# Up products of the last two layers 512 columns wide in pairs of PSUM banks, with fixed banks for the down products

## The chip, the cores and the metric

The kernel runs on one core of a Trainium2 chip. The metric is the device time of one execution in microseconds (us). Engines are PE (TensorE), DVE (VectorE), ACT (ScalarE), POOL (GpSimd) and SP (SyncE, which issues the DMAs).

## What is computed

256 tokens with D = 1024 go through one block with sparse attention, retention and a convolved feed-forward part, and then through a two-layer block with differential attention, a convolution, a Fourier branch and a gated feed-forward part. The change touches the feed-forward parts and the output mixing:

```python
x = x + (gate_a * y_a + gate_b * y_b) @ w_mix_out[layer]   # first block
...
x = x + merged @ w_out[l]                                   # second block, l = 0, 1
h2 = rmsnorm(x, norm2_g[l])
f_gate, f_up = jnp.split(h2 @ w_ffn_in[l], 2, axis=-1)
x = x + (jax.nn.silu(f_gate) * f_up) @ w_ffn_out[l]
```

The feed-forward width is 2816, that is 22 tiles of 128 columns for the gate and 22 for the up part. All data are float32.

## The kernel before

**Precision.** A float32 operand is split into an upper part in a shorter format (`hi`, a copy) and the rest (`lo` = value - `hi`). A product of two such operands is three products of the parts: `hi` by `hi`, `hi` by `lo`, `lo` by `hi`. Weights come from memory in chunks of 128 x 2048 (1 MB), in the order of `PLAN`. For each chunk i, SP loads `raw` (4 buffers), ACT copies it to `whi` (L913, 3 buffers), and DVE subtracts to `wlo` (L1474, 3 buffers). `splits(i + AHEAD)` with AHEAD = 2 puts that work two chunks ahead of PE in the program of ACT and DVE. The upper split of chunk i waits until PE has used chunk i - 3.

**Order.** Each engine has a program of its own (`pe_program`, `act_program`, `dve_program`, `pool_program`, `sp_program`), written in the order in which it runs. Engines wait for one another by named events that stand for values of semaphores. The program is run once in rehearsal to learn these values.

**Banks.** PSUM has eight banks of 512 float32 columns: `pb`, a ring of four that `take_bank` hands out in turn, and four (`sc`, `tp`, `ob`) for scores, transposes and values. `take_bank` makes PE wait until the earlier holder of the bank is freed (event `free`).

**Up stages.** `ffn(n, ...)` runs three times: n = 0 in the first block (`up0`, with a causal convolution), n = 1 and 2 in the second (`up1`, `up2`). Unit f of an up stage is one chunk, which holds the 128 gate columns and the 128 up columns of tile f for all 8 blocks of 128 rows. `feats` (L509 to L511) computes it on PE with the weights as stationary operand and the 256 tokens as moving operand: 8 blocks x 2 halves x 3 products of 256 columns, into one bank, gate in columns 0 to 255 and up part in 256 to 511. For n = 1 and 2, ACT then takes the SiLU of the gate half into `fs` (L1179), and DVE multiplies it by the up half into `fg` (L1880), which frees the bank. ACT makes the upper half `ghi` (L962), and DVE the lower half `glo` (L1507). `fs`, `fg` and `fu` have two buffers each.

For n = 0, ACT copies with scale and bias into `fu` (L1182), DVE does the other taps from PSUM (L1871), which frees the bank, ACT takes the SiLU (L1163), and POOL multiplies (L1389).

**Down stages.** `dn` n has 11 chunks, each of two blocks of 128 rows and all 1024 output columns. Four groups (token half tt by column half hf) accumulate over all 22 blocks, with three products of 512 columns a block each (L456 to L458 in `mul3`). Each group takes a bank of the ring at its first product, so the four groups begin with the banks of the last four up units.

**Mixing.** `yb` has four units f. DVE multiplies by the gate into `gm` (L1829), POOL adds this to `mg` (L1383), ACT makes the upper part `mh` (L962), DVE the lower part `ml` (L1507). Then `to_x` computes the product with `w_mix_out` (`mo`) from rows: PE waits for the event `mixed`, which is set once for the row blocks 0 to 3 and once for 4 to 7. In the second block DVE does that addition (L2076) itself, after the multiplication (L2071); the product there is `out0` and `out1`.

## Time and profile before

| | us |
|---|---|
| median of 3 runs (range) | 1431.55 (1429.74 to 1433.89) |
| the profiled execution's own time | 1431.48 |
| its span, first to last instruction | 1430.2 |

The page gives busy time and share of the span for each engine. The mean granted TensorE clock was 0.981 of full speed. In a timeline row the first number is the start from the beginning of the span, the second the duration, and the brackets at the end give the time in which the engine sat idle before it and what it then waited for. A row without brackets started straight after the one before it on its engine. Successive instructions of one engine overlap a little, so that a start can lie before the end of the one before.

### The profile page before, as it was taken

How to read it: one execution, taken by the hardware profiler on the slowest of the kernel's cores; microseconds unless marked ns; L12 is line 12 of the kernel's file. 1: busy time of each engine (PE TensorE's matmuls, PEld its weight loads, DVE VectorE, ACT ScalarE, POOL GpSimd, SP SyncE). 2: the span in 40 equal slices, each digit the busy share in tenths (PEclk: the TensorE clock that was granted, in tenths of full speed). 3: DMA queues.
4: the chain of work that ended last, by engine and by line, in shares of the span. 5: the costliest groups of instructions: out<-in, count | busy, mean ns of one | idle time of the engine just before them, and what ended most of it. 6: DMA issues, size and time to landing. Idle time of an engine off the chain costs nothing. (4 is left out here: it accounts for less than half of the span.)

```text
span 1430.2 us, 21050 instructions
## 1 busy us (share of the span) xinstructions
PE 1347.8 (94%) x8946; PEld 1218.7 (85%) x8946; DVE 902.4 (63%) x1173; ACT 656.4 (46%) x902; POOL 164.7 (12%) x118
## 2 busy tenths in 40 slices
PE   7999999989998898899998999999889999899999
PEld 6878889889986796678997999879667899799987
DVE  5655465568774559976576555445997657655543
ACT  5634435355553453344644444344334564444432
POOL 0100030113330005200110000000620011000000
PEclk9999999999998999999999999999999999999999
DMA  8643234444554454223344555556322334355551
GB/s 333 220 183 131 89 104 177 176 154 171 177 177 167 158 209 148 88 89 118 126 170 162 179 187 190 181 176 210 147 89 88 118 133 162 148 183 189 189 178 58
DMA packets 33503, 226.49 MB, mean 158 GB/s; under 512 B 3713, under 2 KB 4097, under 8 KB 7425
## 3 DMA queue, kind: packets, MB, share of 16 engines
q1 hardware_dynamic: 33408, 225.14, 43.9%
q8 instruction: 71, 1.16, 0.3%
q14 instruction: 24, 0.19, 0.0%
HBM read 224.08 MB, written 1.05 MB: 157 GB/s over the span
## 5 line engine op out<-in xcount | busy, mean ns | idle before, releaser
L1474 DVE TENSOR_TENSOR wlo<-raw,whi 128x2048 fp32r<-128x2048 f32 x205 | 470.9, 2300 | 305.2 <-ACT whi L913 236.8
L509 PE MATMUL ps<-hhi,whi 128*128 128x256 f32 x1696 | 490.6, 289 | 2.9 <-DVE hlo L1507 2.2
L510 PE MATMUL ps<-hlo,whi 128*128 128x256 f32 x1696 | 483.4, 285 | 0.0
L511 PE MATMUL ps<-hhi,wlo 128*128 128x256 f32 x1696 | 483.2, 285 | 0.0
L913 ACT ACTIVATE whi<-raw 128x2048 fp32r<-128x2048 f32 x205 | 388.7, 1900 | 166.2 <-PE ps L458 146.8
L509 PEld LDWEIGHTS ps<-hhi,whi 128*128 128x128 f32 x1696 | 329.0, 194 | 15.5 <-issue 13.9
L510 PEld LDWEIGHTS ps<-hlo,whi 128*128 128x128 f32 x1696 | 329.3, 194 | 0.4 <-issue 0.2
L511 PEld LDWEIGHTS ps<-hhi,wlo 128*128 128x128 f32 x1696 | 328.9, 194 | 0.0
L1353 POOL TENSOR_TENSOR st<-st,sm 128x1 f32<-128x1 f32 (+2 forms) x30 | 46.2, 1540 | 694.3 <-DVE st L1526 367.3
L456 PE MATMUL ps<-whi,hhi 128*128 128x512 f32 (+1 forms) x272 | 110.9, 408 | 8.2 <-DVE hlo L1507 6.3
L456 PE MATMUL ps<-whi,ghi 128*128 128x512 f32 x264 | 104.2, 395 | 7.1 <-DVE fu L1871 7.0
L1944 DVE SCALAR_TENSOR_TENSOR cv<-gp,sm,cv 128x256 f32<-128x256 f32 x240 | 110.4, 511 | 0.0
L457 PE MATMUL ps<-wlo,hhi 128*128 128x512 f32 (+1 forms) x272 | 107.3, 395 | 0.0
L458 PE MATMUL ps<-whi,hlo 128*128 128x512 f32 (+1 forms) x272 | 107.0, 393 | 0.0
L457 PE MATMUL ps<-wlo,ghi 128*128 128x512 f32 x264 | 103.7, 393 | 0.0
L458 PE MATMUL ps<-whi,glo 128*128 128x512 f32 x264 | 103.7, 393 | 0.0
L1179 ACT ACTIVATE fs<-ps 128x256 f32<-128x256 f32 x44 | 16.9, 383 | 145.3 <-PE ps L511 145.3
L456 PEld LDWEIGHTS ps<-whi,hhi 128*128 128x128 f32 x272 | 52.9, 194 | 21.2 <-DVE wlo L1474 4.0
L1305 ACT ACTIVATE E<-ps,st 128x256 f32<-128x256 f32 x64 | 29.7, 469 | 83.4 <-DVE st L2020 83.4
L456 PEld LDWEIGHTS ps<-whi,ghi 128*128 128x128 f32 x264 | 50.1, 190 | 18.8 <-DVE fu L1871 8.1
L458 PEld LDWEIGHTS ps<-whi,hlo 128*128 128x128 f32 x272 | 52.8, 194 | 11.0
L457 PEld LDWEIGHTS ps<-wlo,hhi 128*128 128x128 f32 x272 | 52.8, 194 | 9.6 <-issue 0.2
(267 smaller groups left out, 1784.4 us busy)
## 6 DMA issues: line engine op xcount, KB each, us to landing
raw<-in_w SPq DMA_DIRECT2D x203, 1024.0 KB, 4.8
gain<-in_rows SPq DMA_DIRECT2D x5, 512.0 KB, 3.7
raw<-in_w SPq DMA_DIRECT2D x8, 256.0 KB, 6.6
raw<-in_w SPq DMA_DIRECT2D x2, 560.0 KB, 8.0
...
```

The source lines that it names most:

```text
L456: pe.op.matmul(o, sh, mh, start=start, stop=False, skip_group_check=True)
L457: pe.op.matmul(o, sh, ml, start=False, stop=False, skip_group_check=True)
L458: signalled(pe.op.matmul(o, sl, mh, start=False, stop=stop, skip_group_check=True), names)
L509: pe.op.matmul(o, wh[:, k, c:c + 128], hi[:, k, :], start=first, stop=False, skip_group_check=True)
L510: pe.op.matmul(o, wh[:, k, c:c + 128], lo[:, k, :], start=False, stop=False, skip_group_check=True)
L511: ins = pe.op.matmul(o, wl[:, k, c:c + 128], hi[:, k, :], start=False, stop=last, skip_group_check=True)
L913: act.op.activation(t.whi[i % NHL][:, 0:n], t.raw[i % NRAW][:, 0:n], ACT.Copy).then_inc(*at("act_hi", ("hi", i)))
L1179: act.op.activation(t.fs[f % 2][:, :], ps[:, 0, :], ACT.Silu).then_inc(*at("act_out", ("fs", n, f)))
L1305: act.op.activation(t.E2[u % 2][:, c, :], t.sc[u % 2][:, c * S:c * S + S], ACT.Exp, bias=nm[:, hd, tt, c:c + 1], accum_out=lw[:, hd, tt, c ...
L1353: pool.op.tensor_tensor(o, a, small(t, "mhalf")[:, 0:a.shape[-1]], ALU.pow).then_inc(*at("pool_small", name))
L1474: dve.op.tensor_tensor(t.wlo[i % NHL][:, c], t.raw[i % NRAW][:, c], t.whi[i % NHL][:, c].bitcast(F32), ALU.subtract).then_inc(*at("dve_lo" ...
L1944: ins = dve.op.scalar_tensor_tensor(t.cv[:, f, :], t.gp[:, f, j:j + S], cw[:, f, j:j + 1], t.cv[:, f, :], ALU.mult, ALU.add)
```

## The change

- In `up1` and `up2` a unit takes a pair of banks, `b` and `b + 1`, with `b = f % 4 * 2`, so four pairs over all eight banks. `hhi` and `hlo` become the halves of one tile `hh`. For each row block and half, one product of the upper weights with both parts of the data (512 columns: columns 0 to 255 by `hhi`, 256 to 511 by `hlo`), and one of the lower weights with `hhi` (256 columns, added to columns 0 to 255).
- ACT copies the two right halves (512 columns) out into `fu`; DVE adds them to the left halves in PSUM (`summed`); ACT then takes the SiLU. The product and its two halves follow, `glo` one unit later than before.
- The four groups of every down stage have banks 4 to 7.
- The addition of `yb` moves from POOL to DVE.
- The event `mixed` is set for each pair of row blocks, for `mo`, `out0` and `out1`.

```diff
@@ -160,14 +160,31 @@
 class Banks:
 
 
+
     def __init__(self, known):
-        self.known, self.turn, self.of, self.holds = known, 0, {}, [None] * 4
+        self.known, self.ring, self.of, self.holds = known, [0, 1, 2, 3], {}, [None] * 8
 
     def take(self, name):
-        b = self.turn % 4
-        self.turn += 1
+        b = self.ring.pop(0)
+        self.ring.append(b)
+        return b, self.fix(name, b)
+
+    def fix(self, name, b):
+
         before, self.holds[b], self.of[name] = self.holds[b], name, b
-        return b, before
+        return before
+
+    def pair(self, name, b):
+
+        return self.fix(name, b + 1), self.fix(name, b)
+
...
 
     def find(self, name):
         return 0 if self.known is None else self.known[name]
@@ -265,8 +282,8 @@
     t.whi = [at(f"whi{i}", 32 + 8 * i, [128, CW], R32) for i in range(NHL)]
     t.wlo = [at(f"wlo{i}", 56 + 8 * i, [128, CW], R32) for i in range(NHL)]
     t.x = at("x", 80, [128, 2, D])
-    t.hhi = at("hhi", 88, [128, 8, S], R32)
-    t.hlo = at("hlo", 96, [128, 8, S], R32)
+    t.hh = at("hh", 88, [128, 2, 8, S], R32)
+    t.hhi, t.hlo = t.hh[:, 0, :, :], t.hh[:, 1, :, :]
     t.gain = at("gain", 104, [128, D])
     t.sm = at("sm", 108, [128, NSMALL])
     p0 = 108 + (NSMALL * 4 + 1023) // 1024
@@ -354,7 +371,8 @@
     t.mg.append(at("mg2", z + 16, [128, 8, S]))
     t.osq = at("osq", y, [128, D])
 
-    t.ps = [ctx.enter_context(nc.psum_tensor(f"ps{i}", [128, 512], F32)) for i in range(8)]
+    t.psum = ctx.enter_context(nc.psum_tensor("ps", [128, 8, 512], F32))
+    t.ps = [t.psum[:, i, :] for i in range(8)]
     t.pb, t.sc, t.tp, t.ob = t.ps[0:4], t.ps[4:6], t.ps[6], t.ps[7]
     return t
 
@@ -513,6 +531,25 @@
                 if last:
                     ins.then_inc(*at("pe_weights", ("got", u, p), *([("used", i)] if p == pairs - 1 else [])))
                 yield
+
+    def wide_feats(u, b, data):
+
+
+        i = UNITS[u][0]
+        wh, wl = weights(i, t.whi[i % NHL]), weights(i, t.wlo[i % NHL])
+        pe.wait_ge(*on("lo", i))
+        for before in pb.pair((u, 0), b):
+            if before:
+                pe.wait_ge(*on("free", before))
+        for k in range(8):
+            for w in data(k):
+                pe.wait_ge(*on(*w))
+            for f in range(2):
+                o, c = t.ps[b + f], slice(f * 128, f * 128 + 128)
+                pe.op.matmul(o[:, :], wh[:, k, c], t.hh[:, :, k, :], start=k == 0, stop=False, skip_group_check=True)
+                ins = pe.op.matmul(o[:, 0:S], wl[:, k, c], t.hhi[:, k, :], start=False, stop=k == 7,
+                                   skip_group_check=True)
+        ins.then_inc(*at("pe_weights", ("got", u, 0), ("used", i)))
 
     def norm_turned(norm, tt):
         for h in range(2):
@@ -729,7 +766,7 @@
     def to_x(u, m, norm):
 
 
-        data = lambda k, tt: ("mixed", u, k // 4)
+        data = lambda k, tt: ("mixed", u, k // 2 * 2)
         run(rows(f"{u}_0" if u != "mo" else "mo0", t.mh[m], t.ml[m], data))
         u1 = f"{u}_1" if u != "mo" else "mo1"
         run(rows(u1, t.mh[m], t.ml[m], data, held_steps(u1, 0), {13: lambda: norm_turned(norm, 0)}))
@@ -741,7 +778,10 @@
     def ffn(n, norm, after, early):
         ev.name("pe_turned", ("up starts", n, "pe"))
         for f in range(NFT):
-            run(feats(f"up{n}_{f}", *h, 8, of_norm_feats(norm)))
+            if n:
+                wide_feats(f"up{n}_{f}", f % 4 * 2, of_norm_feats(norm))
+            else:
+                run(feats(f"up{n}_{f}", *h, 8, of_norm_feats(norm)))
         banks = {}
 
         def down(i, k, kg, tt, hf, ends=()):
@@ -749,9 +789,12 @@
             pe.wait_ge(*on("g", n, kg))
             wh, wl = weights(i, t.whi[i % NHL]), weights(i, t.wlo[i % NHL])
             if kg == 0:
-                banks[tt, hf] = take_bank((f"dn{n}", tt, hf))
+                banks[tt, hf] = 4 + 2 * tt + hf
+                before = pb.fix((f"dn{n}", tt, hf), banks[tt, hf])
+                if before:
+                    pe.wait_ge(*on("free", before))
             ends = list(ends) + ([("got", f"dn{n}", tt, hf)] if kg == NFT - 1 else [])
-            mul3(t.pb[banks[tt, hf]][:, :], t.ghi[:, kg, tok(tt)], t.glo[:, kg, tok(tt)], wh[:, k, half(hf)],
+            mul3(t.ps[banks[tt, hf]][:, :], t.ghi[:, kg, tok(tt)], t.glo[:, kg, tok(tt)], wh[:, k, half(hf)],
                  wl[:, k, half(hf)], kg == 0, kg == NFT - 1, ends)
 
         chunks = UNITS[f"dn{n}"]
@@ -889,7 +932,7 @@
     st = t.st
 
     def bank(name):
-        return t.pb[pb.find(name)]
+        return t.ps[pb.find(name)]
 
     upto = [0]
 
@@ -1164,20 +1207,28 @@
                 *at("act_small", ("fs", n, f)))
 
         def out(f):
+            if n:
+                b = pb.find((f"up{n}_{f}", 0))
+                if f >= 1:
+                    g_upper(f - 1)
+                act.wait_ge(*on("got", f"up{n}_{f}", 0))
+                if f >= 2:
+                    act.wait_ge(*on("summed", n, f - 2))
+                act.op.activation(t.fu[f % 2][:, :, :], t.psum[:, b:b + 2, S:2 * S], ACT.Copy).then_inc(
+                    *at("act_out", ("low part", n, f)))
+                act.wait_ge(*on("summed", n, f))
+                if f >= 2:
+                    act.wait_ge(*on("fg", n, f - 2))
+                act.op.activation(t.fs[f % 2][:, :], t.ps[b][:, 0:S], ACT.Silu).then_inc(*at("act_out", ("fs", n, f)))
+                return
             ps = bank((f"up{n}_{f}", 0))[:, :].rearrange("p (f s) -> p f s", f=2)
-            if n == 0:
-                if f >= 2:
-                    g_upper(f - 2)
-                if f >= 1:
-                    gated(f - 1)
-            elif f >= 1:
-                g_upper(f - 1)
+            if f >= 2:
+                g_upper(f - 2)
+            if f >= 1:
+                gated(f - 1)
             act.wait_ge(*on("got", f"up{n}_{f}", 0))
             if f >= 2:
                 act.wait_ge(*on("g", n, f - 2))
-            if n:
-                act.op.activation(t.fs[f % 2][:, :], ps[:, 0, :], ACT.Silu).then_inc(*at("act_out", ("fs", n, f)))
-                return
             for v in range(2):
                 act.op.activation(t.fu[f % 2][:, v, :], ps[:, v, :], ACT.Identity, scale=fc[:, f, v, 2:3],
                                   bias=fc[:, f, v, 3:4]).then_inc(*at("act_out", *([("fu biased", f)] * v)))
@@ -1376,12 +1427,6 @@
             *at("pool_small", ("sg gained", tt)))
     for k in range(4):
         power(("ret rs", k), st[:, 200 + 2 * k:202 + 2 * k], st[:, 192 + 2 * k:194 + 2 * k], ("ret var", k))
-    for f in range(4):
-        j = 2 * f
-        pool.wait_ge(*on("free", (f"yb{f}", 0)))
-        pool.wait_ge(*on("ya gated", f))
-        pool.op.tensor_tensor(t.mg[0][:, j:j + 2, :], t.mg[0][:, j:j + 2, :], t.gm[4 + f], ALU.add).then_inc(
-            *at("pool_small", ("merged", "mo", j)))
     for tt in range(2):
         norm_power("n1", tt)
     for f in range(NFT):
@@ -1444,7 +1489,7 @@
     upto = [0]
 
     def bank(name):
-        return t.pb[pb.find(name)]
+        return t.ps[pb.find(name)]
 
     def pair(name):
         return bank(name)[:, :].rearrange("p (f s) -> p f s", f=2)
@@ -1818,7 +1863,7 @@
 
     def mixed_lower(u, j, m):
         jj = slice(j, j + 2)
-        lower([("mixed", u, j // 4)] * (j % 4 == 2), t.ml[m][:, jj, :], t.mg[m][:, jj, :], t.mh[m][:, jj, :],
+        lower([("mixed", u, j)], t.ml[m][:, jj, :], t.mg[m][:, jj, :], t.mh[m][:, jj, :],
               ("mixed hi", u, j))
 
     def yb_out(f):
@@ -1828,6 +1873,9 @@
             dve.wait_ge(*on("gm sigmoid", 2))
             dve.op.tensor_tensor(t.gm[4 + f], pair(name), t.gm[4 + f], ALU.mult).then_inc(
                 *at("dve_out", ("free", name)))
+            m = t.mg[0][:, 2 * f:2 * f + 2, :]
+            await_own("dve_out")
+            dve.op.tensor_tensor(m, m, t.gm[4 + f], ALU.add).then_inc(*at("dve_small", ("merged", "mo", 2 * f)))
             mixed_lower("mo", 2 * f, 0)
         return out
 
@@ -1872,18 +1920,35 @@
                                                 ALU.mult, ALU.add).then_inc(*at("dve_out", *ends))
                 await_own("dve_out") if j == 1 else None
 
+        def summed(f):
+
+            b = pb.find((f"up{n}_{f}", 0))
+            dve.wait_ge(*on("low part", n, f))
+            two = t.psum[:, b:b + 2, 0:S]
+            dve.op.tensor_tensor(two, two, t.fu[f % 2][:, :, :], ALU.add).then_inc(
+                *at("dve_out", ("summed", n, f)))
+
         def gated(f):
             name = (f"up{n}_{f}", 0)
-            if f:
-                g_lower(f - 1)
             dve.wait_ge(*on("fs", n, f))
-            dve.op.tensor_tensor(t.fg[f % 2][:, :], pair(name)[:, 1, :], t.fs[f % 2][:, :], ALU.mult).then_inc(
-                *at("dve_out", ("fg", n, f), ("free", name)))
+            dve.wait_ge(*on("summed", n, f))
+            if f >= 2:
+                dve.wait_ge(*on("g hi", n, f - 2))
+            dve.op.tensor_tensor(t.fg[f % 2][:, :], t.ps[pb.find(name) + 1][:, 0:S], t.fs[f % 2][:, :],
+                                 ALU.mult).then_inc(*at("dve_out", ("fg", n, f), ("free", name)))
+
+        def up_out(f):
+            if f >= 1:
+                gated(f - 1)
+            if f >= 2:
+                g_lower(f - 2)
+            summed(f)
 
         for f in range(NFT):
-            run(feats(f"up{n}_{f}", 8, lambda p: gated(f) if n else convolved(f)))
-        if n == 0:
-            g_lower(NFT - 2)
+            run(feats(f"up{n}_{f}", 8, lambda p: up_out(f) if n else convolved(f)))
+        if n:
+            gated(NFT - 1)
+        g_lower(NFT - 2)
         g_lower(NFT - 1)
         chunks = UNITS[f"dn{n}"]
         for i in chunks[:-1]:
```

How the order moves is seen best where a unit follows a unit. ACT at the start of `up1` (suffixes such as `_55` are buffers, brackets hold the semaphores that it waits for), before:

```order
L1179 ACTIVATE fs_124<-ps 128x256 [waits pe_weights]
L913 ACTIVATE whi_55<-raw_51 128x2048 [waits d_raw2]
L962 ACTIVATE ghi<-fg_126 128x256 [waits dve_out]
L1179 ACTIVATE fs_125<-ps 128x256 [waits pe_weights]
L913 ACTIVATE whi_53<-raw_52 128x2048 [waits d_raw3]
L962 ACTIVATE ghi<-fg_127 128x256 [waits dve_out]
```

and in the changed kernel:

```order
L1217 ACTIVATE fu_121<-ps 128x512 [waits pe_weights]
L1222 ACTIVATE fs_123<-ps 128x256 [waits dve_out]
L956 ACTIVATE whi_55<-raw_51 128x2048 [waits d_raw2]
L1005 ACTIVATE ghi<-fg_125 128x256 [waits dve_out]
L1217 ACTIVATE fu_122<-ps 128x512 [waits pe_weights]
L1222 ACTIVATE fs_124<-ps 128x256 [waits dve_out]
L956 ACTIVATE whi_53<-raw_52 128x2048 [waits d_raw3]
L1005 ACTIVATE ghi<-fg_126 128x256 [waits dve_out]
```

The SiLU (L1179, now L1222) waited for PE alone in the first units. It now stands behind a copy of 512 columns (L1217) and waits for DVE (`dve_out`); the upper half of `fg` (`ghi`) stands ahead of the copy.

DVE in the same place, from the first `fg` on, before:

```order
L1880 TENSOR_TENSOR fg_126<-ps,fs_124 128x256 [waits act_out]
L1474 TENSOR_TENSOR wlo_58<-raw_51,whi_55 128x2048 [waits pe_weights,act_hi,d_raw2]
L1507 TENSOR_TENSOR glo<-fg_126,ghi 128x256 [waits act_small]
L1880 TENSOR_TENSOR fg_127<-ps,fs_125 128x256 [waits act_out]
L1474 TENSOR_TENSOR wlo_56<-raw_52,whi_53 128x2048 [waits pe_weights,act_hi,d_raw3]
L1507 TENSOR_TENSOR glo<-fg_127,ghi 128x256 [waits act_small]
L1880 TENSOR_TENSOR fg_126<-ps,fs_124 128x256 [waits act_out]
```

and in the changed kernel, from the sum of unit 1 on:

```order
L1928 TENSOR_TENSOR ps<-ps,fu_122 128x2x256 [waits act_out]
L1519 TENSOR_TENSOR wlo_56<-raw_52,whi_53 128x2048 [waits pe_weights,act_hi,d_raw3]
L1937 TENSOR_TENSOR fg_126<-ps,fs_124 128x256 [waits dve_out,act_out]
L1552 TENSOR_TENSOR glo<-fg_125,ghi 128x256 [waits act_small]
L1928 TENSOR_TENSOR ps<-ps,fu_121 128x2x256 [waits act_out]
L1519 TENSOR_TENSOR wlo_57<-raw_49,whi_54 128x2048 [waits pe_weights,act_hi,d_raw0]
L1937 TENSOR_TENSOR fg_125<-ps,fs_123 128x256 [waits dve_out,act_out]
L1552 TENSOR_TENSOR glo<-fg_126,ghi 128x256 [waits act_small]
```

The sum in PSUM (L1928) is new and stands at the end of each turn, behind the lower split (L1519), `fg` (L1937) and `glo` (L1552).

PE at the first products of `dn0`, before:

```order
L456 MATMUL ps<-whi_55,ghi 128x512 [waits dve_out,dve_small,dve_lo]
L457 MATMUL ps<-wlo_58,ghi 128x512
L458 MATMUL ps<-whi_55,glo 128x512
L456 MATMUL ps<-whi_55,ghi 128x512 [waits dve_out]
L457 MATMUL ps<-wlo_58,ghi 128x512
L458 MATMUL ps<-whi_55,glo 128x512
L456 MATMUL ps<-whi_55,ghi 128x512 [waits dve_out]
L457 MATMUL ps<-wlo_58,ghi 128x512
L458 MATMUL ps<-whi_55,glo 128x512
L456 MATMUL ps<-whi_55,ghi 128x512 [waits dve_out]
```

and in the changed kernel:

```order
L474 MATMUL ps<-whi_55,ghi 128x512 [waits dve_small,dve_lo]
L475 MATMUL ps<-wlo_58,ghi 128x512
L476 MATMUL ps<-whi_55,glo 128x512
L474 MATMUL ps<-whi_55,ghi 128x512
L475 MATMUL ps<-wlo_58,ghi 128x512
L476 MATMUL ps<-whi_55,glo 128x512
L474 MATMUL ps<-whi_55,ghi 128x512
L475 MATMUL ps<-wlo_58,ghi 128x512
L476 MATMUL ps<-whi_55,glo 128x512
L474 MATMUL ps<-whi_55,ghi 128x512
```

The waits for `dve_out` ahead of the four groups, which are waits for banks, are gone; the waits for the data (`dve_small`) and the weights (`dve_lo`) stay.

## Rows read from the trace of the kernel before

**Rows 1.** Page, part 1: busy us and share of the span of each engine.

```profile
PE 1347.8 (94%) x8946; PEld 1218.7 (85%) x8946; DVE 902.4 (63%) x1173; ACT 656.4 (46%) x902; POOL 164.7 (12%) x118
```

**Rows 2.** Busy time by stage: 22 units of second up stage; engines in the page's order.

```profile
776.00:903.00 127.00, 127.00 (x1053) 126.96 (x1053) 68.59 (x65) 54.38 (x66) 0.00 (x0) 0.99 0.51 183
```

**Rows 3.** Timeline, PE, second down stage: start us, us; first and last of 24 products.

```profile
944.78 0.39 PE L456 MATMUL ps<-whi,ghi 128*128 128x512 f32 x1
...
950.00 0.39 PE L458 MATMUL ps<-whi,glo 128*128 128x512 f32 x1
```

**Rows 4.** Timeline, PE and ACT, second up stage: its first product, first SiLU.

```profile
774.52 0.55 PE L509 MATMUL ps<-hhi,whi 128*128 128x256 f32 x1 [0.84 <-DVE hlo L1507]
...
781.84 0.38 ACT L1179 ACTIVATE fs<-ps 128x256 f32<-128x256 f32 x1 [3.93 <-PE ps L511]
```

**Rows 5.** Timeline, ACT, one turn of that stage, eight units later.

```profile
827.91 0.38 ACT L1179 ACTIVATE fs<-ps 128x256 f32<-128x256 f32 x1 [3.27 <-PE ps L511]
...
828.20 1.90 ACT L913 ACTIVATE whi<-raw 128x2048 fp32r<-128x2048 f32 x1
...
830.00 0.41 ACT L962 ACTIVATE ghi<-fg 128x256 fp32r<-128x256 f32 x1
```

**Rows 6.** Timeline, DVE, the same turn.

```profile
830.19 2.29 DVE L1474 TENSOR_TENSOR wlo<-raw,whi 128x2048 fp32r<-128x2048 f32 x1 [1.43 <-ACT whi L913]
...
832.40 0.42 DVE L1507 TENSOR_TENSOR glo<-fg,ghi 128x256 fp32r<-128x256 f32 x1
...
834.09 0.42 DVE L1880 TENSOR_TENSOR fg<-ps,fs 128x256 f32<-128x256 f32 x1 [1.27 <-ACT fs L1179]
```

**Rows 7.** Groups by line and form: xcount, busy us, mean ns; idle before, releaser.

```profile
L1842 DVE TENSOR_TENSOR x<-ps,x 128x512 f32<-128x512 f32 x24 | 16.3, 688 | 16.3 <-PE ps L458 16.3
...
L962 ACT ACTIVATE hhi<-ps 128x512 fp32r<-128x512 f32 x20 | 11.8, 596 | 21.3 <-PE ps L469 20.8
...
L1880 DVE TENSOR_TENSOR fg<-ps,fs 128x256 f32<-128x256 f32 x44 | 18.7, 425 | 56.7 <-ACT fs L1179 56.7
```

**Rows 8.** Timeline, DVE then ACT, before the first out product.

```profile
736.40 0.68 DVE L2071 TENSOR_TENSOR gm<-ps,gm 128x512 f32<-128x512 f32 x1
...
737.19 0.69 DVE L2076 TENSOR_TENSOR mg<-mg,gm 128x512 f32<-128x512 f32 x1
...
737.92 0.63 ACT L962 ACTIVATE mh<-mg 128x512 fp32r<-128x512 f32 x1 [3.83 <-DVE mg L2076]
```

**Rows 9.** Timeline, DVE, POOL, ACT, DVE: one turn of the yb stage.

```profile
253.57 0.68 DVE L1829 TENSOR_TENSOR gm<-ps,gm 128x512 f32<-128x512 f32 x1
...
254.33 1.30 POOL L1383 TENSOR_TENSOR mg<-mg,gm 128x512 f32<-128x512 f32 x1 [5.54 <-DVE gm L1829]
...
255.66 0.63 ACT L962 ACTIVATE mh<-mg 128x512 fp32r<-128x512 f32 x1 [4.41 <-POOL mg L1383]
...
260.41 0.69 DVE L1829 TENSOR_TENSOR gm<-ps,gm 128x512 f32<-128x512 f32 x1
```

**Rows 10.** Timeline, PE: the waits in the mo and out0 products.

```profile
270.83 0.47 PE L456 MATMUL ps<-whi,mh 128*128 128x512 f32 x1 [1.40 <-DVE ml L1507]
...
751.25 0.47 PE L456 MATMUL ps<-whi,mh 128*128 128x512 f32 x1 [2.19 <-DVE ml L1507]
```

**Rows 11.** Timeline, PE then DVE, where the first down stage begins.

```profile
428.86 0.50 PE L456 MATMUL ps<-whi,ghi 128*128 128x512 f32 x1 [2.13 <-DVE fu L1871]
...
435.01 0.79 PE L456 MATMUL ps<-whi,ghi 128*128 128x512 f32 x1 [4.85 <-DVE fu L1871]
...
435.60 0.63 PE L457 MATMUL ps<-wlo,ghi 128*128 128x512 f32 x1
...
439.44 0.44 PE L457 MATMUL ps<-wlo,ghi 128*128 128x512 f32 x1
...
428.87 2.29 DVE L1474 TENSOR_TENSOR wlo<-raw,whi 128x2048 fp32r<-128x2048 f32 x1
...
438.55 2.29 DVE L1474 TENSOR_TENSOR wlo<-raw,whi 128x2048 fp32r<-128x2048 f32 x1 [1.43 <-ACT whi L913]
```

5 lines of the change are left out of this document (added).

## The prediction

> **What bounds the kernel now.** I read the page's busy shares first: PE is busy for 94% of the span, DVE for 63%, ACT for 46% [rows 1]. Then the busy time by stage: in the second up stage (`up1`) PE is busy for all 127 us, DVE for 69, ACT for 54 [rows 2]. On shares alone everything that shortens PE's work there is gain, and DVE and ACT have room. The third view, the timeline, is the one that decides: what counts for DVE and ACT is whether their work for one unit forms a closed ring that is longer than PE's unit. In the up stages of layers 1 and 2 it doesn't now: ACT starts one SiLU 781.84 and another 827.91 [rows 4, 5], eight units apart, so one turn is 5.76 us, which is PE's 48 products of 256 columns at 0.120 us. ACT waited 3.27 us for PE before the SiLU [rows 5]. PE is the bound there.
>
> **The wide products.** A unit of `up1` and `up2` goes from 48 products of 256 columns to 16 of 512 and 16 of 256. The first and the last of 24 products of 512 columns start 5.22 us apart [rows 3], 23 steps of 0.227. So the unit costs PE 16 x 0.227 + 16 x 0.120 = 5.55 us, 0.21 less. Over 44 units that would be 9.4 us, if nothing else set the pace. The strided operand (two runs of 256 columns) has no row of its own; I take the price of the contiguous one, and a PE unit up to 6.6 us long would be hidden by what follows.
>
> **The work behind them.** Now ACT must copy the low halves out (512 columns), DVE must add them to the high halves in PSUM (512 columns), and only then may ACT take its SiLU. Before, a unit needed none of these. This closes a ring, because both engines run in program order: SiLU of f, upper split of the weights of f+3 on ACT, their lower split on DVE, the product `fg` of f on DVE (it stands behind the split in DVE's order), its upper half `ghi` on ACT, then the low copy of f+1, the sum of f+1, the SiLU of f+1. I price each step from start to start. SiLU to upper split: 827.91 to 828.20, 0.29 [rows 5]. Upper to lower split: 828.20 to 830.19, 1.99 [rows 5, 6]. Lower split to the next on DVE: 830.19 to 832.40, 2.21 [rows 6]. `fg` 0.425 [rows 7], plus 0.04 for ACT to follow DVE (737.19 + 0.69 to 737.92) [rows 8]: 0.47. `ghi` 0.41, of which the next ACT instruction overlaps 0.1 as after the split (828.20 + 1.90 against 830.00): 0.31 [rows 5]. Low copy: 0.60 for ACT on 512 columns out of PSUM [rows 7], 0.61 taken since it reads two banks, and 0.03: 0.64. Sum: 0.69 as DVE's other additions of 512 columns from PSUM [rows 7], plus 0.04: 0.73. Together 0.29 + 1.99 + 2.21 + 0.47 + 0.31 + 0.64 + 0.73 = **6.64 us** a turn, 6.62 with unrounded numbers, against PE's 5.55 and against 5.76 before.
>
> The two new prices have no row. Bounds: the low copy costs no less than one ACT read of 256 columns, 0.38 [rows 5], and no more than two, 0.77. The sum, which writes PSUM where every row of DVE writes SBUF, lies between one operation of 256 columns, 0.425, and two, 0.85 [rows 7]; I take the equal width. The 263 ns between 0.688 and 0.425 are the price of 256 columns, so 0.162 are fixed. The Trainium skill (Perfetto Trace Analysis, Optimizing Scalar/DVE Operations) puts DVE's overhead on PSUM at about 125 ns and the profiled latency at about twice the overhead. By it the sum would be an estimated 0.78, the turn 6.71, and the time 4 us later than mine; the same rule gives 0.51 for `fg`, where the row has 0.425, so I stay with the row.
>
> **What the ring costs.** The splits are two units ahead, so PE runs free at first. Times from PE's first product of the stage (774.52 before, rows 4): PE has unit 0 done at 1.40 + 5.55 = 6.95. The 1.40 is the slow start, seen as 7.32 from first product to first SiLU, less 5.76, less the 0.16 in which the last product ends; it stays. The first ring turn begins its upper split (for unit 3) at 6.95 + 0.19 + 0.64 + 0.73 + 0.29 = 8.80, and the lower split ends 4.28 later, 13.08. The weights of unit j are then ready at 13.08 + 6.62 (j - 3), PE wants them at 6.95 + 5.55 (j - 1): late from j = 8 on, by 1.07 each. The last two in the ring are the first two chunks of `dn`: chunk 1 (j = 23) is ready at 145.5. Chunk 2 comes after the last `ghi`, without a new low copy and sum between: its upper split starts at 148.7, its lower ends at 153.0. From there PE is alone on the path, as before. Before, chunk 2 began at 1.40 + 22 x 5.76 + 2 x 5.44 = 139.0. So one stage loses 14.0 us, `up1` and `up2` together **+28.1**. Of what is queued behind: `fg` frees the banks of unit f about 5 us after its SiLU starts, 6 us before PE needs them for f + 4, so the four pairs of banks cost nothing; raw loads follow the lower splits and have a turn of slack more than now.
>
> **The mo and out products.** In the `yb` stage a ring of this kind already stands: its turn is 253.57 to 260.41, 6.84 us [rows 9], above PE's 5.76. The addition moves from POOL (254.33 start, ACT follows at 255.66, 2.09 after the multiplication) to DVE, where mult, add, ACT take 0.79 + 0.73 = 1.52, as they do before `out0` [rows 8]. Turn 6.27. The fourth `yb` is then merged 2.3 us earlier, and PE's wait of 1.40 in the `mo` product [rows 10] goes: **-1.4**. DVE pays 0.69 more per unit, which lies inside that turn. For `out0` PE waited 2.19 us at row block 4 for the last pair of blocks [rows 10]; now it waits only at block 6, six products (1.36 us) later, for the same event. That gives 1.36, in `out1` the same (one more such row): **-2.7**.
>
> **Own banks for down.** Each of the four groups of `dn0` took a bank of the ring of four, and PE waited 2.13 and 4.85 us for the convolutions of units 20 and 21 to free it [rows 11]. With banks 4 to 7 these waits go. Next is the weights: chunk 1's lower split ends at 428.87 + 2.29 = 431.16 and chunk 2's at 438.55 + 2.29 = 440.84 [rows 11], neither moved. So PE does chunk 0 by 430.6, chunk 1 from 431.2 to 436.6, and waits 4.3 us for chunk 2. Chunk 2 starts at 440.9, before at 440.65 + 5.54 = 446.2: 5.3 us. But in the old wait the clock fell: 435.01 to 435.60 and on to 439.44 the products are nearly twice as far apart (0.43 each, granted clock 0.5, that is 1.2 GHz). Eleven products cost some 2.3 us there, and a wait of 4.3 us should fall alike. So **-3.0**, bounds -3.0 and -5.3. In `dn1` and `dn2` no bank was waited for: nothing.
>
> **Sum.** 28.1 - 1.4 - 2.7 - 3.0 = +21 us. The profiled execution took 1431.48 us, like the median of 1431.55, so **1452 us**.
>
> **Rivals.** (a) *The ring is hidden, the change is faster.* If the turn were under 5.55, all of the PE gain would stand: 9.4 + 1.4 + 2.7 + 3.0 = 16.5, so 1415 us. For it: DVE and ACT are busy for half of the stage [rows 2]. Against: it needs 1.07 less out of seven steps, and the two unknown prices at their lower bounds give only 0.49. The point where it decides is a turn of 6.15 (each 0.1 of turn is 2.2 us a stage): below it the gains outweigh. The chance of a gain over 0.3%, with this or a milder cause, is 0.06.
> (b) *The sum or the low copy is dearer*, as PSUM is read and written at once, in two banks: sum 0.85 and copy 0.77 make a turn of 6.94, +14 us, 1466. Chance 0.12.
> (c) *They are cheaper*: 0.55 and 0.55, turn 6.42, 1443. Chance 0.06, and 0.03 more for a turn so near 6.15 that nothing is seen.
> (d) *The clock.* PE now stops about 1.07 us in every turn. At 1.2 GHz a unit takes 16 x 0.43 + 16 x 0.21 = 10.3 us. If the clock is low for more than a fifth of the work, PE overtakes the ring as bound; at a third a unit is 7.1, and the time 1484. Against it: after lone waits of 1.40 and 2.19 PE restarts with products of 0.47 us, not the 0.79 that follows the long one [rows 10, 11]. The Trainium skill (TensorE: Matmul & The Clock Gate, A second HAM failure mode) tells of a kernel whose short idles between groups made the clock swing between its levels. By that rule this is what would come; this trace shows the fall around waits of 2.13 and 4.85 in ten microseconds [rows 11], and none at a lone 1.40 [rows 10]. Chance 0.05.
>
> **How the numbers follow.** Forecast 0.68, rivals as given. 0.3% is 4.3 us, about what a measurement tells here. Slower: 0.68 + 0.12 + 0.06 + 0.05 = 0.91; same 0.03; faster 0.06. The range takes in (b) nearly whole and (c), 1442 to 1466; it leaves out (a), (d) and the tail.
>
> **What would show it.** In the changed profile: PE's products of 512 columns 0.227 apart; the stage's ACT line for the SiLU no longer waiting for PE but for the sum on DVE; SiLU starts 6.6 us apart; PE waiting about 1.07 us for `wlo` from the ninth unit of `up1` and `up2` on; the wait for `fu` in `dn0` replaced by one for `wlo`; and no POOL row in `mg` for `mo`. A turn of 5.55 with ACT waiting for PE would prove me wrong, and so would a granted clock well below 1 in those stages.

## The result and the profile after

The changed kernel takes 1457.16 us (median of 4 runs, 1456.29 to 1458.22), the kernel before, in runs on the same chip, 1431.01 (4 runs, 1429.74 to 1433.89). The ratio is 1.018 with a 95% interval of 1.0163 to 1.0198. The span of the profiled execution is 1456.5 us, 26.3 more than before. The forecast was 1452, in a range of 1442 to 1466.

The page's busy line of the changed kernel, which answers to [rows 1], with the page's order of engines:

```profile
PE 1356.6 (93%) x8242; PEld 1184.7 (81%) x8242; DVE 931.2 (64%) x1221; ACT 682.6 (47%) x946; POOL 159.2 (11%) x114
```

PE is busy about as long as before in spite of 704 fewer products, which shows that the busy share says little. In a turn of 6.61 us in which it waited 0.8 us it counts as busy for 5.8 us, where its 32 products need 5.55: the product behind the wait takes 0.10 us more to the next, and the last one, modelled at 0.28 us, is not overlapped by the product that would follow after 0.12. The same 127 us of `up1` by engine (the columns of [rows 2]):

```profile
770.00:897.00 127.00, 118.66 (x651) 100.11 (x651) 70.02 (x74) 58.02 (x76) 0.00 (x0) 0.99 0.46 162
```

PE now has 8 us without work in the stage whose whole length it filled before. DVE is busy for only 70 of 127 us and ACT for 58, and yet they set the pace. The timeline shows how. ACT in one turn, start and duration first, from one SiLU to the next:

```profile
823.58 0.38 ACT L1222 ACTIVATE fs<-ps 128x256 f32<-128x256 f32 x1 [0.77 <-DVE ps L1928]
823.86 1.91 ACT L956 ACTIVATE whi<-raw 128x2048 fp32r<-128x2048 f32 x1
828.52 0.42 ACT L1005 ACTIVATE ghi<-fg 128x256 fp32r<-128x256 f32 x1 [2.75 <-DVE fg L1937]
828.84 0.58 ACT L1217 ACTIVATE fu<-ps 128x512 f32<-128x512 f32 x1
830.19 0.39 ACT L1222 ACTIVATE fs<-ps 128x256 f32<-128x256 f32 x1 [0.77 <-DVE ps L1928]
```

and DVE in the same turn:

```profile
825.86 2.29 DVE L1519 TENSOR_TENSOR wlo<-raw,whi 128x2048 fp32r<-128x2048 f32 x1 [2.31 <-ACT whi L956]
828.07 0.42 DVE L1937 TENSOR_TENSOR fg<-ps,fs 128x256 f32<-128x256 f32 x1
828.40 0.41 DVE L1552 TENSOR_TENSOR glo<-fg,ghi 128x256 fp32r<-128x256 f32 x1
829.46 0.70 DVE L1928 TENSOR_TENSOR ps<-ps,fu 128x512 f32<-128x512 f32 x1 [0.64 <-ACT fu L1217]
```

The turn is 830.19 - 823.58 = 6.61 us. Each row but `glo` waits for the one before it in the ring or starts as soon as that lets it: SiLU, upper split, lower split (DVE idle 2.31 for it), `fg`, `ghi` (ACT idle 2.75), low copy, sum (DVE idle 0.64), SiLU (ACT idle 0.77). Both engines stand still for part of each turn, one for the other. Three new or changed groups, with count, busy time, mean ns, and idle before:

```profile
L1217 ACT ACTIVATE fu<-ps 128x512 f32<-128x512 f32 x44 | 25.6, 582 | 9.3 <-PE ps L550 9.3
...
L1928 DVE TENSOR_TENSOR ps<-ps,fu 128x512 f32<-128x512 f32 x44 | 30.8, 700 | 32.5 <-ACT fu L1217 32.5
...
L1222 ACT ACTIVATE fs<-ps 128x256 f32<-128x256 f32 x44 | 16.9, 385 | 33.7 <-DVE ps L1928 33.7
```

SiLU waits for DVE (33.7 us) and no longer for PE. PE's own rows show the first wait in the tenth unit (f = 9) of both stages. First that wait in `up1` and the next, then the second and the third chunk of `dn1`, and products behind the third:

```profile
821.60 0.50 PE L549 MATMUL ps<-hh,whi 128*128 128x512 f32 x1 [0.45 <-DVE wlo L1519]
...
828.21 0.50 PE L549 MATMUL ps<-hh,whi 128*128 128x512 f32 x1 [0.78 <-DVE wlo L1519]
...
914.11 0.50 PE L474 MATMUL ps<-whi,ghi 128*128 128x512 f32 x1 [0.86 <-DVE wlo L1519]
...
921.63 0.50 PE L474 MATMUL ps<-whi,ghi 128*128 128x512 f32 x1 [1.78 <-DVE wlo L1519]
...
922.48 0.63 PE L474 MATMUL ps<-whi,ghi 128*128 128x512 f32 x1
922.91 0.63 PE L475 MATMUL ps<-wlo,ghi 128*128 128x512 f32 x1
```

The last two rows are 0.43 us apart, the pace of 1.2 GHz: after the wait of 1.78 us the granted clock fell, and it stayed so for some eight products. PE's waits for the weights in `up1` and `up2` together, as who waited, for whom, total, times, longest:

```profile
PE ps L549 <- DVE wlo L1519: 18.3, 26, 0.8
```

**Where the 26.3 us are.** I cut PE's timeline of both kernels at the first or last product of each stage and compare lengths. The starts are from the traces, the differences are mine:

| from | to | before | after | difference |
|---|---|---|---|---|
| span start | first `mo` product | 263.81 | 263.46 | -0.35 |
| first `mo` product | first of `up0` | 30.26 | 28.60 | -1.66 |
| first of `up0` | first of `dn0` | 130.99 | 130.74 | -0.25 |
| first of `dn0` | last of `dn0` | 69.79 | 67.46 | -2.33 |
| last of `dn0` | first `out0` product | 248.58 | 247.24 | -1.34 |
| first `out0` product | first of `up1` | 31.09 | 30.79 | -0.30 |
| first of `up1` | last of `dn1` | 188.60 | 204.72 | **+16.12** |
| last of `dn1` | first `out1` product | 244.39 | 245.66 | +1.27 |
| first `out1` product | first of `up2` | 31.08 | 29.69 | -1.39 |
| first of `up2` | last of `dn2` | 187.79 | 204.34 | **+16.55** |

The two stages with the ring cost 32.7 us, and everything else gives back 6.35. Of that, 5.68 lies in the four segments that the change was to shorten (`mo`, `dn0`, `out0`, `out1`), and 0.67 is what is left of gains and losses in the other four, where no gain was looked for.

### The profile page after: what moved, and what is told of

Same layout as the page of the kernel before. It is cut to its first block and busy times, and to the rows that moved or that the text cites. A ratio compares the mean times of both kernels' runs of the same rounds, so it can differ in the third digit from the quotient of the medians.

```text
span 1456.5 us, 19733 instructions
## 1 busy us (share of the span) xinstructions
PE 1356.6 (93%) x8242; PEld 1184.7 (81%) x8242; DVE 931.2 (64%) x1221; ACT 682.6 (47%) x946; POOL 159.2 (11%) x114
## 5 line engine op out<-in xcount | busy, mean ns | idle before, releaser
L1519 DVE TENSOR_TENSOR wlo<-raw,whi 128x2048 fp32r<-128x2048 f32 x205 | 470.3, 2299 | 331.1 <-ACT whi L956 263.0
L527 PE MATMUL ps<-hh,whi 128*128 128x256 f32 x992 | 289.9, 292 | 1.0 <-DVE hh L1552 0.6
L528 PE MATMUL ps<-hh,whi 128*128 128x256 f32 x992 | 283.0, 285 | 0.0
L529 PE MATMUL ps<-hh,wlo 128*128 128x256 f32 x992 | 282.9, 285 | 0.0
L549 PE MATMUL ps<-hh,whi 128*128 128x512 f32 x704 | 255.8, 406 | 20.2 <-DVE wlo L1519 18.3
L527 PEld LDWEIGHTS ps<-hh,whi 128*128 128x128 f32 x992 | 192.5, 194 | 13.2 <-issue 11.9
L550 PE MATMUL ps<-hh,wlo 128*128 128x256 f32 x704 | 199.0, 283 | 0.0
L528 PEld LDWEIGHTS ps<-hh,whi 128*128 128x128 f32 x992 | 192.9, 194 | 0.4 <-issue 0.2
L529 PEld LDWEIGHTS ps<-hh,wlo 128*128 128x128 f32 x992 | 192.6, 194 | 0.0
L549 PEld LDWEIGHTS ps<-hh,whi 128*128 128x128 f32 x704 | 134.1, 191 | 61.1 <-DVE wlo L1519 26.6
L550 PEld LDWEIGHTS ps<-hh,wlo 128*128 128x128 f32 x704 | 134.9, 192 | 0.0
L474 PE MATMUL ps<-whi,hh 128*128 128x512 f32 (+1 forms) x272 | 112.0, 412 | 8.1 <-DVE hh L1552 6.3
L475 PE MATMUL ps<-wlo,hh 128*128 128x512 f32 (+1 forms) x272 | 107.8, 396 | 0.0
L476 PE MATMUL ps<-whi,hh 128*128 128x512 f32 (+1 forms) x272 | 107.8, 396 | 0.0
L1005 ACT ACTIVATE ghi<-fg 128x256 fp32r<-128x256 f32 x66 | 27.4, 415 | 117.3 <-DVE fg L1937 116.4
```

Of the source, the lines that this page charges most:

```text
L474: pe.op.matmul(o, sh, mh, start=start, stop=False, skip_group_check=True)
L475: pe.op.matmul(o, sh, ml, start=False, stop=False, skip_group_check=True)
L476: signalled(pe.op.matmul(o, sl, mh, start=False, stop=stop, skip_group_check=True), names)
L527: pe.op.matmul(o, wh[:, k, c:c + 128], hi[:, k, :], start=first, stop=False, skip_group_check=True)
L528: pe.op.matmul(o, wh[:, k, c:c + 128], lo[:, k, :], start=False, stop=False, skip_group_check=True)
L529: ins = pe.op.matmul(o, wl[:, k, c:c + 128], hi[:, k, :], start=False, stop=last, skip_group_check=True)
```

## The experiments

All ratios are to the kernel before, in runs on the same chip.

**The order on DVE.** The ring is closed by one thing: `fg` of a unit stands behind the lower split of unit f + 3. The edit turns that, in `up1` and `up2` (it also drops the product of the last unit behind the loop, which is no longer needed there; that part is not shown):

```diff
         def up_out(f):
-            if f >= 1:
-                gated(f - 1)
-            if f >= 2:
-                g_lower(f - 2)
             summed(f)
+            gated(f)
+            if f >= 1:
+                g_lower(f - 1)
```

> The changed kernel with DVE's order inside a unit of up1 and up2 turned: sum of f, product fg of f, glo of f - 1, and only then the lower split of f + 3. Ring theory: the product and ghi leave the ring, which is now sum to SiLU 0.73, SiLU to upper split 0.29, upper to lower split 1.99, lower split to the next sum 2.21, together 5.22 us, under PE's 5.55. So the turn is 5.55, SiLU waits for PE's unit again, PE never waits for the weights in these stages, and the time is that of rival (a), 1415 us, up to 1420 if the clock falls after the norms as it does now. Rival: the wide products or the sharing of PSUM are slow by themselves; then the turn stays near 6.6 and the time near 1457.

Measured: 1419.96 us, ratio 0.9922 (0.9903 to 0.994). It does the same work with the same instructions, and is 1457.2 - 1420.0 = 37 us faster than the changed kernel. DVE from split to split, and ACT's next copy:

```profile
802.09 2.29 DVE L1519 TENSOR_TENSOR wlo<-raw,whi 128x2048 fp32r<-128x2048 f32 x1 [1.10 <-issue]
804.62 0.70 DVE L1928 TENSOR_TENSOR ps<-ps,fu 128x512 f32<-128x512 f32 x1 [0.24 <-ACT fu L1217]
805.77 0.42 DVE L1937 TENSOR_TENSOR fg<-ps,fs 128x256 f32<-128x256 f32 x1 [0.45 <-ACT fs L1222]
806.11 0.42 DVE L1552 TENSOR_TENSOR glo<-fg,ghi 128x256 fp32r<-128x256 f32 x1
807.63 2.29 DVE L1519 TENSOR_TENSOR wlo<-raw,whi 128x2048 fp32r<-128x2048 f32 x1 [1.10 <-issue]
...
809.54 0.60 ACT L1217 ACTIVATE fu<-ps 128x512 f32<-128x512 f32 x1 [1.69 <-PE ps L550]
```

The turn is 807.63 - 802.09 = 5.54 us, PE's unit, and ACT waits 1.69 us for PE before the low copy. PE has no wait for weights left in `up1` and `up2`. So the wide products can run at 5.54 us a unit, as rows of plain 512 column products had promised. The rival, that the wide products or the sharing of PSUM are slow by themselves, is out: the order on DVE made the loss.

The time is 5 us over the 1415 of rival (a). Half of that lies in `up2`, whose unit is longer. From SiLU to SiLU on ACT it is 1300.25 - 1294.60 = 5.65 us there:

```profile
1294.60 0.39 ACT L1222 ACTIVATE fs<-ps 128x256 f32<-128x256 f32 x1 [0.77 <-DVE ps L1928]
...
1300.25 0.39 ACT L1222 ACTIVATE fs<-ps 128x256 f32<-128x256 f32 x1 [0.77 <-DVE ps L1928]
```

0.11 us more in each of 22 units is 2.4 us. PE doesn't wait in these units, its granted clock is 1.00, and its products of 512 columns are 0.235 us apart and not 0.227. The turned order is not the cause. The changed kernel has both paces in one and the same stage: in `up1` its third unit, which waits for nothing, takes 787.07 - 781.41 = 5.66 us in the first trace, and 788.23 - 782.68 = 5.55 in a second trace of the same program (described below). First the first trace:

```profile
781.41 0.40 PE L549 MATMUL ps<-hh,whi 128*128 128x512 f32 x1
...
787.07 0.40 PE L549 MATMUL ps<-hh,whi 128*128 128x512 f32 x1
```

then the second:

```profile
782.68 0.40 PE L549 MATMUL ps<-hh,whi 128*128 128x512 f32 x1
...
788.23 0.40 PE L549 MATMUL ps<-hh,whi 128*128 128x512 f32 x1
```

So the pace differs between executions of one kernel, and between stages of one execution. What sets it stays open.

**The size of one link.** The sum made twice (with the low parts added twice), and the sum cut to 8 columns of each half (the rest of the low parts left out):

```diff
+            dve.op.tensor_tensor(two, two, t.fu[f % 2][:, :, :], ALU.add).then_inc(*at("dve_out"))
+            await_own("dve_out")
             dve.op.tensor_tensor(two, two, t.fu[f % 2][:, :, :], ALU.add).then_inc(
```

```diff
-            two = t.psum[:, b:b + 2, 0:S]
-            dve.op.tensor_tensor(two, two, t.fu[f % 2][:, :, :], ALU.add).then_inc(
+            two = t.psum[:, b:b + 2, 0:8]
+            dve.op.tensor_tensor(two, two, t.fu[f % 2][:, :, 0:8], ALU.add).then_inc(
```

> The changed kernel with the sum in PSUM made twice in each unit of up1 and up2 (the low parts are added twice). Ring theory: DVE's second sum starts 0.8 us after the first and lies wholly in the ring, so the turn is 7.41 and the loss 17.6 us a stage, 35 in all: 1492 us. Rival, PE bound by its own wide products: DVE is busy for 58% of the stage, and 44 sums of 0.7 us would be hidden: 1457.

> The changed kernel with the sum in PSUM over 8 columns of each half in place of 256 (the low parts of the other columns are left out). Ring theory: the sum falls from 0.70 to about 0.2 us, the turn from 6.61 to 6.1, 11 us less a stage: 1435 us. Rival as before: unchanged at 1457.

Measured: 1487.22 us (ratio 1.0397, 1.0381 to 1.0414) and 1431.9 us (1.0007, 0.9997 to 1.0018). First DVE's rows with the sum twice, from one sum to the next turn's:

```profile
829.41 0.70 DVE L1928 TENSOR_TENSOR ps<-ps,fu 128x512 f32<-128x512 f32 x1 [0.64 <-ACT fu L1217]
830.15 0.70 DVE L1930 TENSOR_TENSOR ps<-ps,fu 128x512 f32<-128x512 f32 x1
...
836.75 0.70 DVE L1928 TENSOR_TENSOR ps<-ps,fu 128x512 f32<-128x512 f32 x1 [0.64 <-ACT fu L1217]
```

and with the short sum:

```profile
829.87 0.18 DVE L1928 TENSOR_TENSOR ps<-ps,fu 128x16 f32<-128x16 f32 x1 [0.64 <-ACT fu L1217]
...
835.95 0.18 DVE L1928 TENSOR_TENSOR ps<-ps,fu 128x16 f32<-128x16 f32 x1 [0.63 <-ACT fu L1217]
```

The turns are 7.34 and 6.08 us against 6.61. The second sum began 0.74 us after the first, not 0.80, and the turn grew by 0.73. The short sum took 0.18 instead of 0.70, and the turn shrank by 0.53. The link's length passes into the turn one to one in both directions, and that into the time: +30 and -25 us for 44 units. That excludes a bound on PE. Expected were 1492 and 1435 us. The first is 5 us off, since the second sum follows after 0.74 us and not 0.80 (some 3 us in 44 units), and since the clock didn't fall in `dn2`. The second is 3 us off, since with a wait of 1.2 to 1.3 us at chunk 2 the clock fell in neither stage.

With the sum twice PE waits 1.42 to 1.52 us in every turn from unit 7 on, and the granted clock stays at 1.00 there. At chunk 2 it then waits 2.51 us in `dn1`, and the clock falls. In `dn2` it waits 2.50, and the next products are 0.34 and 0.23 us apart, at full clock:

```profile
1435.20 0.50 PE L474 MATMUL ps<-whi,ghi 128*128 128x512 f32 x1 [2.50 <-DVE wlo L1519]
1435.54 0.39 PE L475 MATMUL ps<-wlo,ghi 128*128 128x512 f32 x1
1435.77 0.39 PE L476 MATMUL ps<-whi,glo 128*128 128x512 f32 x1
```

The short sum also shows where the break-even turn is: at 6.08 us the kernel takes what it took before.

**The rest of the change without the wide products.**

> The kernel before with the other parts of the change alone: banks 4 to 7 for the down products, the yb addition on DVE, and the event mixed for each pair of row blocks. The up stages stay as before. Prediction's terms: -3.0 -1.4 -2.7 = -7.1, 1424 us. By the trace of the changed kernel (dn0 -2.3, mo -1.9, out0 -0.3, out1 -1.4) -5.9, 1425 us. Rival: what PE saves in a wait is given back in the next, as the clock falls or another wait ends last: 1429 to 1431.

The edit is the diff of the change without its parts in `wide_feats`, in ACT's `out` and in DVE's `up_out`. Measured: 1426.07 us, ratio 0.9965 (0.9952 to 0.9978), that is 5.0 us (3.1 to 6.9) under the kernel before. The expectation was 1424 to 1425. Against the changed kernel this leaves 31 us for the wide products in the changed kernel's order.

**Each of the two parts alone.**

> The kernel before with banks 4 to 7 for the down products and nothing else. Prediction's term: PE's waits for the convolutions of units 20 and 21 go, a wait of 4.1 to 4.3 us for the weights of chunk 2 takes their place, and the clock falls in it as in the old one: -3.0 (bounds -3.0 and -5.3), 1428 us. The trace of the changed kernel gives -2.3 for this stage. Rival: given back whole, 1431.

> The kernel before with the yb addition on DVE and the event mixed for each pair of row blocks, and nothing else. Prediction's terms: -1.4 in mo, -1.36 each in out0 and out1, 1427 us. In the changed kernel 1.1 of out0's gain was lost at once, since the clock fell one group of transposes earlier; if that is a matter of where the clock's fall happens to lie and not of the change, it comes and goes with the run, and the gain lies between 3 and 4.3.

Measured: banks alone 1431.09 us over 11 runs, ratio 0.9995 (0.9984 to 1.0007), so no gain that can be seen, at most 2.3 us. Mixing alone 1428.9 us, 0.9981 (0.9972 to 0.999), 2.7 us (1.4 to 4.0). Their sum is under the 5.0 us of both together, but the intervals are too wide to say that the parts don't add up. The second is under its expected 3 to 4.3, but its mechanism is there. Its `yb` ring has a turn of 6.19 us where 6.27 was forecast, on DVE:

```profile
252.32 0.68 DVE L1823 TENSOR_TENSOR gm<-ps,gm 128x512 f32<-128x512 f32 x1
253.03 0.69 DVE L1827 TENSOR_TENSOR mg<-mg,gm 128x512 f32<-128x512 f32 x1
...
258.51 0.68 DVE L1823 TENSOR_TENSOR gm<-ps,gm 128x512 f32<-128x512 f32 x1
```

The first misses its 1428 and is at the rival's 1431, given back whole: the trace of the banks alone shows `dn0` shorter by 3.44 us (66.35 against 69.79), and 1.56 us more from `out0` to `up1`, 1.44 more in `up1`, 1.26 more from `dn1` to `out1`, 0.79 more from `dn0` to `out0`. None of these has an instruction that the edit touches. What differs is the time at 1.2 GHz after the waits that stand there anyway.

**How long the clock stays low.** At the start of `up1` PE has waited 3.3 us for the norm. Granted clock is the third column from the end; first the kernel before, then the changed kernel, both in steps of 4 us from 6 us before the first product:

```profile
768.50:772.50 4.00, 0.69 (x4) 0.30 (x3) 1.93 (x4) 0.72 (x2) 0.56 (x1) 1.00 0.00 0
772.50:776.50 4.00, 3.12 (x17) 2.71 (x17) 2.04 (x4) 3.39 (x4) 0.00 (x0) 0.69 0.36 131
776.50:780.50 4.00, 4.00 (x32) 4.00 (x31) 4.00 (x2) 1.41 (x1) 0.00 (x0) 0.88 0.17 39
```

```profile
762.30:766.30 4.00, 1.26 (x7) 1.08 (x8) 1.79 (x4) 1.14 (x3) 0.56 (x1) 0.88 0.00 0
766.30:770.30 4.00, 2.50 (x9) 1.83 (x8) 2.37 (x3) 3.66 (x4) 0.00 (x0) 0.50 0.39 131
770.30:774.30 4.00, 4.00 (x20) 3.43 (x19) 3.51 (x2) 0.71 (x1) 0.00 (x0) 0.77 0.40 129
```

The wait is the same, but the time at 1.2 GHz is not. A granted clock of 0.69 over 4 us means that 62% of them passed at half of full speed, so the rows give 2.5 + 1.0 = 3.5 us before and 1.0 + 4.0 + 1.8 = 6.8 us after, some 3 more: the clock fell already during the transposes. From these to the first product it took 3.26 us and not 2.14, and most of what `mixed` had won in `out0` was gone. To see if this is the kernel's or the single execution's, three kernels were traced again unchanged.

> The kernel before, unchanged, for a second trace of it. In the traces so far the stretch at 1.2 GHz at the start of up1 was 4 us long in the kernel before and 5 to 7 in nine others. Theory A, its length is a matter of the single execution: here it differs from 4, and segments between restarts move by 1 us or so against the first trace. Theory B, it is fixed by the kernel: 4 again, all segments within 0.3.

> The banks alone, unchanged, for a second trace. In the first, dn0 gained 3.4 us and the segments out0 to up1, up1 to dn1, dn1 end to out1 and dn0 end to out0 lost 1.6, 1.4, 1.3 and 0.8. Theory A (chance of one execution): other places lose, dn0 gains again 2 to 3.5. Theory B: the same losses at the same places.

> The changed kernel, unchanged, for a second trace. The turn in up1 and up2 must be 6.61 again, and PE's wait at down chunk 2 1.9 us. Theory A: the clock's fall after it comes in one of the two stages and not in the other, or with another length. Theory B: as in the first trace, 1.8 us lost in both stages.

Lengths in us between the cuts of the table above, first and second trace:

| | `dn0` | `dn0` to `out0` | `out0` to `up1` | `up1` | `dn1` to `out1` | `dn2` |
|---|---|---|---|---|---|---|
| before | 69.79, 69.56 | 248.58, 248.50 | 31.09, 31.06 | 128.08, 128.04 | 244.39, 244.38 | 59.65, 59.64 |
| banks alone | 66.35, 66.34 | 249.37, 248.08 | 32.65, 31.03 | 129.52, 129.36 | 245.65, 245.61 | 59.64, 59.65 |
| changed | 67.46, 66.37 | 247.24, 249.57 | 30.79, 30.43 | 139.21, 139.63 | 245.66, 245.70 | 64.61, 63.01 |

The result is mixed. Theory B (fixed by the kernel) holds for the kernel before and for two places of the banks alone: `up1` and the stretch from `dn1` to `out1` are 1.3 us longer both times. Theory A (the single execution) holds for `dn0` to `out0`, where the changed kernel moves by 2.3 us, for its `dn0` (1.1), for `out0` to `up1` of the banks alone (1.6), and for `dn2`. In `dn2` the clock fell after the wait at chunk 2 in one trace and not in the other, though the wait was the same. So gains of 1 to 3 us can be given back at a later wait, as they were here. Why the kernel before has the short form at those places both times stays open.

**The waits at down chunk 2.** On the kernel with the turned order, the splits of chunk 2 go ahead of the last halves of `g`:

```diff
+        chunks = UNITS[f"dn{n}"]
+        splits(chunks[0] + AHEAD)
         if n == 0:
             g_upper(NFT - 2)
             gated(NFT - 1)
         g_upper(NFT - 1)
-        chunks = UNITS[f"dn{n}"]
```

and likewise on DVE ahead of `g_lower`.

> The kernel with DVE's turned order, and in each feed-forward part the splits of down chunk 2 moved ahead of the last ghi and glo on ACT and DVE. In dn0 the upper split can then start straight after the last copy with bias, about 3.5 us earlier, and the lower split after the last tap. Theory (the new wait in dn0 is for the weights, and the clock falls in it): PE's wait goes from 4.1 to under 1 us and the clock stays up, 3.5 + 2.0 = 5.5 us, 1414.5. Rival: the clock falls all the same, or chunk 2's raw data are late: 1416 to 1420.

Measured: 1413.66 us, ratio 0.9877 (0.9859 to 0.9894). PE at chunks 1 and 2 of `dn0` in the changed kernel, start, duration and wait:

```profile
428.98 0.50 PE L474 MATMUL ps<-whi,ghi 128*128 128x512 f32 x1 [0.40 <-DVE wlo L1519]
...
438.68 0.79 PE L474 MATMUL ps<-whi,ghi 128*128 128x512 f32 x1 [3.96 <-DVE wlo L1519]
...
439.27 0.63 PE L475 MATMUL ps<-wlo,ghi 128*128 128x512 f32 x1
```

and with the early split:

```profile
428.81 0.50 PE L474 MATMUL ps<-whi,ghi 128*128 128x512 f32 x1 [0.40 <-DVE wlo L1520]
...
434.99 0.50 PE L474 MATMUL ps<-whi,ghi 128*128 128x512 f32 x1 [0.44 <-DVE wlo L1520]
```

The wait for chunk 2 falls from 3.96 to 0.44 us, and the restart is 0.50 long and not 0.79, as at full clock. `dn0` is 61.26 us long instead of 67.46: 6.2 where 5.5 were expected. Against the trace of the turned order there is one more gain that the edit didn't make: `up2` runs at 5.55 us a unit in this execution.

**The ring of up0.** On top of that:

```diff
             if f >= 2:
-                act.wait_ge(*on("g", n, f - 2))
+                act.wait_ge(*on("fg", n, f - 2))
...
         pool.wait_ge(*on("fs", 0, f))
+        if f >= 2:
+            pool.wait_ge(*on("g", 0, f - 2))
```

> As the run with the early split, and in up0 ACT's copy with bias for unit f waits for POOL's product of f - 2 instead of DVE's glo of f - 2 (POOL waits for that glo in its place). up0 has a ring of its own now: lower split 2.21, glo 1.05, copies with bias 1.05, taps 1.86, together 6.17 a unit. With glo out of the path between ACT and DVE the copies run beside DVE's split, and PE's 5.76 is the bound: up0 3 us shorter and the waits at the first chunks of dn0 gone, 4 us less, 1410.5. Rival: POOL waits for DVE and slows the ring itself, no gain.

Measured: 1409.74 us, ratio 0.9851 (0.9835 to 0.9867), the lowest median of this study: 21 us under the kernel before and 47 under the changed one. ACT's copies with bias are 5.76 us apart and wait for PE; in the kernel with the early split they were 6.18 apart. `dn0` is down to 59.64 us, as long as `dn2` was before:

```profile
380.94 1.02 ACT L1233 ACTIVATE fu<-ps,sm 128x256 f32<-128x256 f32 x2 [2.33 <-PE ps L529]
...
386.70 1.02 ACT L1233 ACTIVATE fu<-ps,sm 128x256 f32<-128x256 f32 x2 [2.33 <-PE ps L529]
```

The ring of `up0` is gone, but its worth in time is not shown. On PE `up0` is 0.74 us shorter (expected: 3) and `dn0` 1.62, together 2.4, since PE ran ahead of the ring for most of that stage. The medians differ by 3.9 us, with overlapping intervals. The two profiled executions are as good as equally long (spans of 1411.2 and 1411.3 us): the one with the new edit ran `up1` and `up2` at 5.65 us a unit, the other ran both at 5.55.

## Why the prediction was right

- **What bounds the kernel.** Right: busy shares of 54% and 43% for DVE and ACT in the stage did not mean room, and the ring did. The turn was forecast at 6.62 us and is 6.61. The order turned shows that it is the ring, the doubled and the short sum that this link counts in full, up and down. The other links were not changed one by one.
- **The prices without a row.** The sum was put at 0.69 and took 0.700; the low copy at 0.61 and took 0.582. The estimate by the Trainium skill (Perfetto Trace Analysis, Optimizing Scalar/DVE Operations), 0.78 for the sum, was too high by 0.08 here. By the rows, 0.700 with the result in PSUM against 0.688 with it in SBUF, writing PSUM costs DVE 12 ns more.
- **The wide products.** 5.55 us a unit were forecast from products with a contiguous operand; 5.54 were measured with two runs of 256 columns in `up1` of the turned order. In other stages and executions a unit took 5.65, among them the free units of the changed kernel's first trace; no term of the forecast had this.
- **When PE begins to wait.** Forecast from unit 8 on. So it is in `up1` of the second trace (0.23 us there); in `up2` and in the first trace it is one unit later, where the free units took 5.65 us and PE came that much later itself. Then PE waited 0.68 to 0.79 us in each turn, so its start was late by some 0.9, where 1.07 was forecast. The turn is as forecast: of its 1.07 over PE's unit some 0.10 lies in the first product after the wait, which takes 0.34 us to the next one and not 0.23, and is no wait in the rows.
- **What the ring costs.** This is the term that was mis-sized: 14.0 us a stage were forecast, 16.1 and 16.5 were measured. Chunk 2 of `dn1` started 153.34 us after the first product of `up1`, forecast 153.04, and in `up2` and `dn2` 153.86 (second trace: 153.76 and 154.14). That is the sum of turns, 0.3 to 1.1 us too short. The other 1.8 us a stage lie behind it: the clock fell after the wait of 1.78 us, and eight products took 0.2 us more each. In `dn2` of the second trace it didn't fall, and the stage cost 15.3 us. The forecast had the clock as a rival for the repeated waits inside the stage. Of these none made it fall; after the longer wait at the end it did, in three of four stages traced. The forecast had worked that wait out (153.0 against 145.5 + 5.4, a wait of 2.1) and had put no price of the clock on it. In the kernel with the short sum that wait is 1.26 us in `dn1`, and the products behind it are 0.23 apart, as they are behind the 2.50 us shown above; so the length of this one wait doesn't decide alone:

```profile
908.69 0.50 PE L474 MATMUL ps<-whi,ghi 128*128 128x512 f32 x1 [1.26 <-DVE wlo L1519]
...
909.49 0.39 PE L474 MATMUL ps<-whi,ghi 128*128 128x512 f32 x1
...
909.72 0.40 PE L475 MATMUL ps<-wlo,ghi 128*128 128x512 f32 x1
```

- **Mixing.** -1.4 and -2.7 were forecast, -1.66, -0.30 and -1.39 measured in the trace. The waits went as forecast (none is left in `mo`, and 0.74 us in `out0`), and the missing 1.1 us of `out0` went to the clock. Alone it gained 2.7 us in the time.
- **Own banks.** -3.0 was forecast, -2.3 and -3.4 are in the two traces of `dn0`, with the forecast wait for the weights in its place (3.96 us, forecast 4.3) and the clock's fall. But alone the banks gained nothing in the time. That `dn0`'s gain would be handed back at later restarts was not in the forecast.
- **Sum.** +28.1 - 7.1 = +21 was forecast; +32.7 - 6.35 = +26.3 was measured, of the 6.35 only 5.7 in the segments that the forecast named. Nearly all of the difference is the term of the ring.
- **The rivals.** (a) is the kernel with the turned order, which does what (a) said, at 1420 us and not 1415. (b) and (c) are out by the measured durations. (d) as told, a rule of the Trainium skill (TensorE: Matmul & The Clock Gate, A second HAM failure mode), did not come in the stages: with a wait of about 0.8 us in every 6.6 the granted clock stayed 1.00 in steps of 50 us from 800 to 900, and it did so with 1.4 to 1.5 us in every 7.3 in the kernel with the sum twice.
